# Feed-forward down products: a ring of four resident activation chunks instead of whole exchanges, and weight sums ahead of low parts

## The reference

```python
    h2 = rmsnorm(x, g_ffn[l]) * (1 + sc2) + sh2
    gate, up = jnp.split(jnp.dot(h2, w_gu[l]), 2, axis=-1)
    x = x + g2 * jnp.dot(jax.nn.silu(gate) * up, w_down[l])
    ...
    y = rmsnorm(x, g_final)
```

## Time and profile before

| | us |
|---|---|
| median of three runs | 2617.49 |
| lowest and highest run | 2616.70, 2619.95 |
| the profiled execution, its time | 2613.09 |
| the profiled execution, its span | 2611.0 |
| TensorE matmuls busy | 2428.4 (93%) |
| VectorE busy | 1562.9 (60%) |
| ScalarE busy | 936.7 (36%) |
| GpSimd (POOL) busy | 186.3 (7%) |

### The profile page before, as it was taken

The page is one execution under the profiler, slowest core; times in us unless marked ns, Lnnn a source line. Parts: engine busy times, 40 slices in busy tenths (PEclk is TensorE's granted clock), DMA queues, the critical chain, the costliest instruction groups (busy, mean ns, idle before and its releaser), DMA issues.

```text
span 2611.0 us, 43931 instructions
## 1 busy us (share of the span) xinstructions
PE 2428.4 (93%) x18485; PEld 2215.3 (85%) x18485; DVE 1562.9 (60%) x2258; ACT 936.7 (36%) x1311; POOL 186.3 (7%) x212
## 2 busy tenths in 40 slices
PE   5789999999999899769999999999999989899996
PEld 1189887777777699769999999999999989899885
DVE  0332442323232332388888878888888778688788
ACT  1122331313131322254444444444444333333333
POOL 3150230000000011100000000000000000000121
PEclk8889999999999999989999999999999989999998
DMA  9954464545454333203354333443344762722622
GB/s 328 333 185 148 137 158 158 182 146 182 145 182 146 119 113 113 103 33 128 132 177 165 127 141 145 157 157 128 127 166 167 299 245 98 313 99 110 253 74 93
DMA packets 185123, 418.49 MB, mean 160 GB/s; under 512 B 13476, under 2 KB 118740, under 8 KB 181088
## 3 DMA queue, kind: packets, MB, share of 16 engines
q1 hardware_dynamic: 174720, 345.25, 38.6%
q0 software_dynamic: 7904, 65.97, 6.4%
q10 hardware_dynamic: 2304, 4.46, 0.4%
HBM read 357.65 MB, written 57.98 MB: 159 GB/s over the span
## 4 chain that ended last, share of the span: by engine, by line
PE 84%; DVE 6%; DMA 5%; issue 3%; ACT 2%; SPq 0%; POOL 0%; DVEq 0%; ACTq 0%; POOLq 0%
PE PJ L1742 25%; PE PJ L2043 24%; PE PS L2043 24%; DMA AR<-in_weights 3%; PE PJ L1695 2%; PE PS L1965 2%; DMA act_parts<-SQ 1%; PE PS L1972 1%; PE PJ L1685 1%; ACT WO L1016 1%; PE PS L1992 1%; DVE W L1503 1%; PE PS L1985 1%; DVE GR L1499 1%; DVE WO L1480 1%
## 5 line engine op out<-in xcount | busy, mean ns | idle before, releaser
L2043 PE MATMUL PJ<-HS,WO 128*128 128x272 f32 x5544 | 719.9, 292 | 76.2 <-DVE HS L1608 28.8
L2043 PEld LDWEIGHTS PJ<-HS,WO 128*128 128x128 f32 x5544 | 712.1, 191 | 80.8 <-issue 47.6
L2043 PE MATMUL PS<-HS,WO 128*128 128x272 f32 x5544 | 705.0, 288 | 5.9 <-DVE W L1503 5.1
L1480 DVE TENSOR_TENSOR WO<-GR,WO 128x1024 fp32r<-128x1024 f32 (+1 forms) x476 | 567.9, 1193 | 234.3 <-ACT WO L1016 233.6
L2043 PEld LDWEIGHTS PS<-HS,WO 128*128 128x128 f32 x5544 | 699.6, 188 | 7.9 <-DVE W L1503 6.0
L1016 ACT ACTIVATE WO<-GR 128x1024 fp32r<-128x1024 f32 (+1 forms) x476 | 490.5, 1034 | 557.7 <-DVE GR L1488 144.5
L1742 PE MATMUL PJ<-HH,WH 128*128 128x272 f32 x1632 | 365.4, 306 | 20.7 <-issue 7.9
L1742 PE MATMUL PJ<-HL,WH 128*128 128x272 f32 x1632 | 341.4, 291 | 0.0
L1742 PE MATMUL PJ<-HH,WL 128*128 128x272 f32 x1632 | 341.1, 291 | 0.0
L1742 PEld LDWEIGHTS PJ<-HH,WH 128*128 128x128 f32 x1632 | 258.1, 192 | 73.3 <-issue 61.1
L1134 DVE TENSOR_TENSOR WL<-RW,WH 128x1024 fp32r<-128x1024 f32 x102 | 126.7, 1247 | 293.1 <-ACT WH L763 292.8
(11 more groups left out here) (269 smaller groups left out, 1647.5 us busy)
## 6 DMA issues: line engine op xcount, KB each, us to landing
GR<-in_weights SPq DMA_DIRECT2D x264, 512.0 KB, 6.8
AR<-in_weights SPq DMA_DIRECT2D x256, 256.0 KB, 4.5
RW<-in_weights SPq DMA_DIRECT2D x102, 512.0 KB, 4.5
act_parts<-SQ SPq DMA_DIRECT2D x44, 952.0 KB, 7.4
AR<-in_weights SPq DMA_DIRECT2D x64, 512.0 KB, 5.4
HS<-act_parts POOLq DMA_DIRECT2D x14, 2176.0 KB, 17.0
HS<-act_parts POOLq DMA_DIRECT2D x7, 1632.0 KB, 11.6
MIX<-in_xT SPq DMA_DIRECT2D x1, 4352.0 KB, 16.8
```

Source lines behind the costliest of these rows:

```text
L1480: d.tensor_tensor(split_part(n, 1), operand(n), split_part(n, 0).bitcast(F32), ALU.subtract)\
L2043: mm = e.matmul(out, w[part], HS[:, QUARTER[i], y, k, :], start=OPENS[i] and k == 0 and x == 0, stop=k == tiles - 1 and x == 2, skip_group ...
```

## The change

The resident chunks become a ring. A virtual chunk number v runs from 0 to 13, where v and v mod 11 are the same chunk; it lies in place v % 4 of HS. A down step works on the chunks lo to up-1 that `chunks(s)` gives: with j = t // 2 and odd = t % 2, r = 0 takes j to j+2+odd, r = 1 the next four, r = 2 the rest up to j+10. Each output tile pair still meets all 11 chunks once. The number of chunks is 3, 4, 3, 4, ... in r = 0, four in all of r = 1, and 4, 3, 4, 3, ... in r = 2. Chunk v is loaded into its place by seven loads of 544 KB (`load_parts`), load i after product i of the last step that uses chunk v-4 (`last_use`). At FT the first three chunks are loaded quarter by quarter, then the fourth. SyncE's extra wait stays only at FT-1.

`XQ` loses its group dimension. The squares of the last norm have one buffer QXF instead of two, and QXF, ACF, RNF and PR lie at other addresses, because all of HS stays in use. In VectorE's slot the sums stand ahead of the low part. The diff, without the moved address lines:

```diff
+def chunks(s):
+
+    if s < FT:
+        return 0, FC
+    r, t = divmod(s - FT, DOWN)
+    j, odd = t // 2, t % 2
+    return ((j, j + 3 + odd), (j + 3 + odd, j + 7 + odd), (j + 7 + odd, j + 11))[r]
+
+
 def slots(s):
 
-    return 4 if s < FT else min(4, NFC - 4 * ((s - FT) // DOWN))
-def group(s):
-
-    return (s - FT) // DOWN
+    lo, up = chunks(s)
+    return up - lo
+
+
+def last_use(v):
+
+    return max(s for s in range(FT, STEPS) if chunks(s)[0] <= v < chunks(s)[1])
...
-    return [V_FFN + V_CHUNK * (4 * group(s) + j) + 4 * FC + (s - FT) % DOWN for j in range(slots(s))]
+    return [V_FFN + V_CHUNK * (v % NFC) + 4 * FC + (s - FT) % DOWN for v in range(*chunks(s))]
...
-    XQ = nc.dram_tensor("act_parts", (3, 7, P, 2, KT // 2, HT), F32).ap()
+    XQ = nc.dram_tensor("act_parts", (7, P, 2, 2 * NFC, HT), F32).ap()
...
-                sp.dma_start(XQ[c // 4, :, :, part, 2 * (c % 4) + j, :].rearrange("q p n -> p q n"),
+                sp.dma_start(XQ[:, :, part, 2 * c + j, :].rearrange("q p n -> p q n"),
...
-                if s >= FT - 1 and (s + 1 - FT) % DOWN == 0:
+                if s == FT - 1:
                     sp.wait_ge(S["w_used"], OPS * (s + 1))
...
-        def load_quarter(s, i):
-
-            g0, n = group(s + 1), 2 * slots(s + 1)
+        def load_parts(s, i, v):
+
             if i == 0:
-                g.wait_ge(S["parts_out"], 64 * min(4 * g0 + 4, NFC))
+                g.wait_ge(S["parts_out"], 64 * min(v + 1, NFC))
+            if v >= 3:
+                g.wait_ge(quarter_in[i], 16 * v)
             g.wait_ge(S["w_used"], OPS * s + i + 1)
-            g.dma_start(HS[:, QUARTER[i], :, 0:n, :].bitcast(F32), XQ[g0, QUARTER[i], :, :, 0:n, :])\
+            at, c = 2 * (v % 4), 2 * (v % NFC)
+            g.dma_start(HS[:, QUARTER[i], :, at:at + 2, :].bitcast(F32), XQ[QUARTER[i], :, :, c:c + 2, :])\
                 .then_inc(quarter_in[i], 16)
...
+        g.wait_ge(S["w_used"], OPS * (FT - 2))
+        load_x1(0)
+        for i in range(OPS):
+            for v in range(3):
+                load_parts(FT - 1, i, v)
+            if i == 5:
+                g.wait_ge(S["af_lo"], 3 * (2 * NFC - 1))
+                load_x1(1)
+        for i in range(OPS):
+            load_parts(FT - 1, i, 3)
+        g.wait_ge(S["parts_out"], 64 * NFC)
+        for v in range(4, 3 + NFC):
+            if v in (4, 5):
+                g.wait_ge(S["w_used"], OPS * (FT + v - 4) + 5)
+                load_x1(v - 2)
+            if last_use(v - 4) >= STEPS - DOWN:
+                break
             for i in range(OPS):
-                load_quarter(s, i)
...
+                load_parts(last_use(v - 4), i, v)
         g.wait_ge(S["w_used"], OPS * (STEPS - DOWN))
         g.memset(ACF[:, :], 0.0).then_inc(S["x1_acc"], 1)
-        for k in range(KT - 1):
-            add_square(1, k, ACF, QXF)
+        for u in range(DOWN):
+            if u:
+                add_square(1, 2 * u - 1, ACF, QXF)
+            for v in range(11, 14):
+                if last_use(v - 4) == STEPS - DOWN + u:
+                    for i in range(OPS):
+                        load_parts(STEPS - DOWN + u, i, v)
+            add_square(1, 2 * u, ACF, QXF)
...
-            a.wait_ge(S["x1_acc"], r * KT + max(k, 1))
-            q = (QXF if r else QX)[k % 2]
+            a.wait_ge(S["x1_acc"], KT + k + 1 if r else max(k, 1))
+            q = QXF if r else QX[k % 2]
...
-            if OPS * s + i + 2 < OPS * STEPS:
-                lo_op(OPS * s + i + 2)
             if i < 3:
                 combine(s, i + 1)
             elif i == 5 and s + 1 < STEPS:
                 combine(s + 1, 0)
+            if OPS * s + i + 2 < OPS * STEPS:
+                lo_op(OPS * s + i + 2)
...
-            if s >= FT and (s - FT) % DOWN == 0:
-                e.wait_ge(quarter_in[i], 16 * (group(s) + 1))
+            first, last = chunks(s)
+            if s == FT or s > FT and last > chunks(s - 1)[1]:
+                e.wait_ge(quarter_in[i], 16 * last)
...
-                    mm = e.matmul(out, w[part], HS[:, QUARTER[i], y, k, :], start=OPENS[i] and k == 0 and x == 0,
+                    mm = e.matmul(out, w[part], HS[:, QUARTER[i], y, (2 * first + k) % (KT // 2), :], start=OPENS[i] and k == 0 and x == 0,
```

More of the change, by code:

```diff
@@ L219, in sb @@
         return nc.alloc_sbuf_tensor_at(name, shape, dt, offset=at)
-    PR = sb("PR", [P, PRM["c"][0]])
     SC = sb("SC", [P, 32])
     TB = sb("TB", [P, 1])
+    pr_at = spot[0]
+    PR = sb("PR", [P, PRM["c"][0]])
     mod_at = spot[0]
@@ L327, in program @@
     RN = sb("RN", [P, NT])
-    QXF = [sb(f"QXF{i}", [P, NT], at=hs_at + i * part_b + 6 * half_b) for i in range(2)]
-    ACF, RNF = (sb(n, [P, NT], at=hs_at + i * part_b + 6 * half_b) for n, i in (("ACF", 2), ("RNF", 3)))
+    RNF = sb("RNF", [P, NT], at=hs_at)
     GR = [sb(f"GR{i}", [P, 4, HU], at=at) for i, at in enumerate((ar_at, wh_at))]
@@ L339, in program @@
     assert hs_end + 4 * HU + 2 * half_b <= wh_at and dead_at + 12 * HU <= dead_end
+    QXF = sb("QXF", [P, NT], at=wh_at + 12 * HU)
+    ACF = sb("ACF", [P, NT], at=mod_at + KT * NSEQ * 4 - tile_b)
+    assert mod_at + KT * NSEQ * 4 - tile_b >= pr_at + 4 * PRM["b_ada"][0]
+    assert all(slots(s) == 3 for s in range(STEPS - DOWN + 1, STEPS, 2))
     assert k_at == ar_at + 16 * HU and k_at + 8 * HU + 2 * half_b <= x1_at
@@ L701, in _, with add_square @@
             g.dma_start(X1[:, k:k + 4, :], ins["xT"][:, k:k + 4, :]).then_inc(x1_in[k // 4], 16)
-        def add_square(r, k, acc, sq):
+        def add_square(r, k, acc, square):
             g.wait_ge(S["x1_sq"], r * KT + k + 1)
             g.wait_ge(S["x1_acc"], r * KT + k + 1)
-            g.tensor_tensor(acc[:, :], acc[:, :], sq[k % 2][:, :], ALU.add).then_inc(S["x1_acc"], 1)
+            g.tensor_tensor(acc[:, :], acc[:, :], square[:, :], ALU.add).then_inc(S["x1_acc"], 1)
         g.wait_ge(S["h_lo"], 2 * KT)
@@ L710, in _ @@
         for k in range(KT - 1):
-            add_square(0, k, AC, QX)
+            add_square(0, k, AC, QX[k % 2])
         g.wait_ge(S["mod_scaled"], 5)
@@ L733, in load_x1 @@
             g.dma_start(X1[:, lo:up, :], XD[:, lo:up, :]).then_inc(x1_in[n], 16)
[L735 to L738, removed]
-            for i in range(OPS):
-                load_quarter(s, i)
[L741 to L748, removed]
+        g.wait_ge(S["w_used"], OPS * (FT - 2))
[15 more added lines that the diff above has]
+                break
+            for i in range(OPS):
+                load_parts(last_use(v - 4), i, v)
         g.wait_ge(S["w_used"], OPS * (STEPS - DOWN))
         g.memset(ACF[:, :], 0.0).then_inc(S["x1_acc"], 1)
-        for k in range(KT - 1):
-            add_square(1, k, ACF, QXF)
+        for u in range(DOWN):
[6 more added lines that the diff above has]
+            add_square(1, 2 * u, ACF, QXF)
     @block.scalar
@@ L2051, in _ @@
         e.wait_ge(S["x1_sq"], 2 * KT)
-        sum_squares(PJ, ACF, QXF[1])
+        sum_squares(PJ, ACF, QXF)
 def t5_buckets():
```

## The result

| | before | after |
|---|---|---|
| median, us | 2617.68 (4 runs) | 2580.59 (4 runs) |
| lowest and highest, us | 2616.70, 2619.95 | 2578.45, 2584.24 |
| the profiled execution, us | 2613.09 | 2578.98 |
| its span, us | 2611.0 | 2576.9 |

The ratio of after to before is 0.9859, 95% interval 0.9841 to 0.9876: 37 us less, where 38 were forecast. The median of 2580.59 us lies 1.1 us from the forecast of 2579.5. The two profiled executions lie closer together, 34.1 us apart, so against them the sum of the terms was 3.9 us too large. That the medians agree to 1.1 us is luck in part: the execution profiled before lay 4.6 us under its median, the one after only 1.6.

What follows compares the result with a forecast made beforehand. TensorE bounds four-chunk steps; all else is loss. Terms 11.7 + 5.7 + 18.5 + 1 + 1.1 = 38.0 us off 2613.09 give 2575.1, plus 4.4 to the median: 2579.5; range 2568 to 2598.

Steps and rivals of the forecast that it cites:

- Exchanges two and three go: Later whole swaps of the resident chunks: replaced by hidden one-chunk refills, saving 11.7 and 5.7 us.
- The cover: One step between a refill's loads and its use hides it; without that step each refill would cost its landing time.
- Three-chunk steps, -18.5: Down steps of three chunks: sums ahead of low parts free VectorE's waits, saving 18.5 us of 21.0 lost.
- The circle of high part and sum: VectorE waits for ScalarE's high part, which needs VectorE's later sum; breaking this frees up to 2.17 us a step.
- First exchange, -1: Chunk loading at FT: the same bytes must be in before FT+1, which starts at 2104; 1 us saved.
- The second rival: At FT, the store lands sooner beside smaller loads and weights follow: 9 us more saved, 2570.5; chance 0.13.
- The last part, 0: Last norm's squares, with QXF a single buffer: no change expected, bounds 0 and +2 us.
- First feed-forward step, -1.1: First feed-forward step: the sum falls into VectorE's wait of 2.14 us, saving 1.1 us.
- the first (VectorE stays the bound in three-chunk steps): Rival for three-chunk steps: VectorE still sets their pace, gain 8 us less, 2588, or 2598 at worst; chance 0.20.
- The third (small loads don't overlap): Rival for POOL's chunk loads: 28 at 4.9 us each delay FT+1, +62 us, 2641.5; chance 0.05.
- The rule against the change: Trainium skill's advice of 1 MiB DMA batches: 28 loads would take 92 us, shrinking the gain to about 18 us.

Runs made afterwards that it cites:

- weights first: Changed kernel with the last activation parts split in FT+1 and FT+1's weights issued ahead of the store, without the wait; down part 488.2 us, ratio 0.9843.
- ring only: Changed kernel with VectorE's low part ahead of the sum again, as before; down part 503.6 us, ratio 0.9918.
- refills without cover: Changed kernel with all seven loads of each r = 1 refill issued only after the old chunk's last step; down part 517.3 us, ratio 0.9970.
- last parts later: Changed kernel with the last activation parts split in FT+1 and their store behind FT+2's weight group; down part 493.9 us, ratio 0.9878.
- store first: Changed kernel with POOL holding the loads from quarter 4 on until the store of parts has landed; down part 487.3 us, ratio 0.9860.

## Why the prediction was right

Point by point, in the spans of the two profiled executions, 34.1 us apart.

- *Exchanges two and three go*: right in full. 11.7 and 5.7 us are gone, and no step of r = 1 waits for a refill. The cover was named rightly: without it a refill costs 7 us, but some 5 of them are the landing and some 2 the slow clock behind it, which the prediction didn't name.
- *Three-chunk steps, -18.5*: right in kind, 1.7 too large. What is left is 2.8 us from FT+1 to the start of the last step (2.5 allowed). The term failed on the other side: it took 18.44 us for all the steps before, but the first behind the third exchange took 17.06 (2461.74 to 2478.80), so there was 1.4 us less to win. The reason given was too simple too. The circle of high part and sum is harmless in r = 0 and costs 3.5 us a pair in r = 2: the same 5.0 us of waits in a pair, which matter only where POOL's adds have filled VectorE's time.
- *First exchange, -1*: right, -0.4. What it takes over its floor is 36.07 - 15.82 = 20.25 us, 20.6 before. The working gave 2104 for the start of FT+1 and it was 2103.88, with the weights in at 2101.37 (2101.5 assumed). The second rival was half there: the store landed 27.7 us after its issue instead of 33.8, and product 5 followed, but the weights then took its place. One step of the working is too strong. All four chunks needn't be in before the first product of FT+1: with the fourth chunk's loads held until the weights were in, FT+1 started 3.2 us sooner and didn't stall, and with the weights first 5.5 us sooner. The bytes set the time for the order in which this kernel asks for them, not for every order.
- *The last part, 0*: right. The wait for QXF at the end is 2.00 us as before (2.06).
- *First feed-forward step, -1.1*: right in kind, -0.7. TensorE's timeline before and after, the first product and the one from which two run on, shows it.

```profile
1108.16 4.89 PE L2043 MATMUL PJ<-HS,WO 128*128 128x272 f32 x24 [14.62 <-DVE HS L1608]
...
1138.03 8.26 PE L2043 MATMUL PJ<-HS,WO 128*128 128x272 f32 x48 [8.09 <-DVE HS L1608]
```

```profile
1108.97 4.76 PE L2071 MATMUL PJ<-HS,WO 128*128 128x272 f32 x24 [14.91 <-DVE HS L1635]
...
1138.14 8.45 PE L2071 MATMUL PJ<-HS,WO 128*128 128x272 f32 x48 [5.38 <-DVE HS L1635]
```

From one to the other it is 29.87 us before and 29.17 after; 29.9 with the ring only, and 29.15 to 29.17 in each of the twelve profiles with the new order. The missing 0.4 us of the term went to POOL, which was at work beside the sum. POOL's timeline before and after:

```profile
1117.91 2.87 POOL L718 TENSOR_TENSOR X<-X,MOD 128x256 f32<-128x256 f32 x1 [12.43 <-DVE X L1602]
```

```profile
1118.73 4.01 POOL L732 TENSOR_TENSOR X<-X,MOD 128x256 f32<-128x256 f32 x1 [12.43 <-DVE X L1629]
```

VectorE's timeline after, which answers to the earlier trace rows:

```profile
1120.97 1.22 DVE L1519 TENSOR_TENSOR GR<-GR 128x1024 f32<-128x1024 f32 x1
1123.61 1.23 DVE L1507 TENSOR_TENSOR WO<-GR,WO 128x1024 fp32r<-128x1024 f32 x1 [1.42 <-POOL X L734]
```

The sum at 1120.97 stands beside POOL's multiply, which now takes 1.14 us longer, and the low part, which waits for POOL in the program, goes on after 1.42 us, where 2.14 less the sum would have left 1.0. The multiply took 4.0 us in each of the kernels with the new order and 2.87 in the one with the ring only.

The 3.9 us by which the sum of terms misses the spans are so 1.7 from the steps of three chunks, 0.6 from the first exchange, 0.4 from this step, and some 1.3 where nothing was meant to change: TensorE came 0.8 us later to its first feed-forward product (0.5 of that already ahead of the last sum of squares before it), lost 0.2 in the last two products of that step, and took 0.3 longer behind the last down step.

Of the rivals, the first (VectorE stays the bound in three-chunk steps) is what the ring alone would have met in r = 2; the reorder was needed against it. The second is half true, as said. The third (small loads don't overlap) is refuted by the refills without cover. The rule against the change was priced a little off in itself: by the third rival's own working its 92 us would have left 38 - 17 = 21 us of gain, not 18.

## What to carry to other kernels

A buffer exchanged whole stalls the engine twice, for the bytes and for the slow clock behind the idle time; replacing one of its four chunks at a time, a step ahead of its use, removed both at 27% more bytes loaded (14 chunks for 11). Where an engine alternates between making another engine's operand and waiting for its result, put the operand first, but look at what else runs in the slot that it moves to: here the order was worth nothing in one stage and 3.5 us a pair in another, and in a third POOL took 0.4 of its 1.1 us. At a crowded exchange, removing the wait that is named last can just move the gap to the next one, as it did with the last parts later and with the store first; holding back what is needed last (the fourth chunk) gave 3.2 us by itself. Count the bytes that must be in before the step and compare with the time that they take, but for each order that they can be asked for in.

## What the runs showed of the hardware beyond that

- VectorE and POOL hold each other up in both directions. A pass of 0.96 us on VectorE took 2.11 beside an add on POOL, and POOL's multiply took 4.01 us instead of 2.87 with one more sum on VectorE beside it, and 0.68 at 1104.86, in the same profile. The Trainium skill, "SBUF — State Buffer", Terms, names a port pair that the two share and that is held for a whole instruction; the 1.14 us agree with it, as that sum takes 1.22.
- After some 5 us of idle time the granted clock was 0.50 over the next 3 us of matmuls in three of the four cases and 0.56 in the fourth, which made the step behind it 1.5 to 2.6 us longer.
- A store of 1.95 MB took, from its issue to ScalarE's going on, 33.8 us beside loads of 2176 KB, 27.7 beside loads of 544 KB and 15.1 with the later loads held back, where 7.4 us is the middle for each of its halves over all 44.
